# Mixture-of-experts decoder step on one core: where TensorE turns the next tile's gathered rows

## The reference, cut to what matters

```python
def hier_moe(h, rw1, rb1, rw2, rb2, w_gate, w_up, w_down):
    t = h.reshape(n * L, D)                       # D = 1024
    ...                                           # gates: two of 16 experts a token
    a = jnp.einsum('td,edf->tef', t, w_gate)      # f = 256
    b = jnp.einsum('td,edf->tef', t, w_up)
    hid = (jax.nn.silu(a) * b * gates[:, :, None].astype(a.dtype)).astype(t.dtype)
    out = jnp.einsum('tef,efd->td', hid, w_down)
    return out.reshape(n, L, D)
```

## Time and profile before

| | before |
|---|---|
| device time, three runs | 1176.96, 1177.94, 1178.39 us; median 1177.94 |
| span of the profiled execution | 1181.0 us |
| TensorE busy | 1083.1 us, 92% |
| VectorE busy | 777.0 us, 66% |
| ScalarE busy | 508.2 us, 43% |
| POOL busy | 295.5 us, 25% |
| the expert loop | about 728 to 1131 us |

### The profile page before, as it was taken

How to read it: one execution, slowest core, us unless ns; L and a number is a source line. 1 busy time by engine, 2 the same in 40 slices (tenths; PEclk the granted TensorE clock), 3 DMA queues, 4 the chain that set the end, 5 groups by cost and what they waited for, 6 DMA issues and landing times. The chain is left out here.

```text
span 1181.0 us, 18306 instructions
## 1 busy us (share of the span) xinstructions
PE 1083.1 (92%) x5541; PEld 804.7 (68%) x5542; DVE 777.0 (66%) x1276; ACT 508.2 (43%) x715; POOL 295.5 (25%) x359
## 2 busy tenths in 40 slices
PE   4799999999958899999999989999999999999992
PEld 2357777676646667777787646787878777778760
DVE  5456575756879973369887778555666555555385
ACT  5133242421132325436665344555555444444373
POOL 0046262616041000030000002333333323333344
PEclk9799999999989999999999989999999999999996
DMA  9834646557677459485766456897789777775597
GB/s 285 304 107 119 194 138 180 147 155 218 195 212 143 145 157 234 175 232 204 250 221 223 162 214 236 238 289 220 214 255 281 214 213 216 214 212 108 111 356 304
DMA packets 169247, 244.77 MB, mean 207 GB/s; under 512 B 66240, under 2 KB 124384, under 8 KB 167088
## 3 DMA queue, kind: packets, MB, share of 16 engines
q1 hardware_dynamic: 140833, 171.06, 45.8%
q0 software_dynamic: 16112, 54.88, 18.3%
q10 hardware_dynamic: 12246, 18.14, 4.6%
HBM read 169.36 MB, written 75.84 MB: 208 GB/s over the span
## 5 line engine op out<-in xcount | busy, mean ns | idle before, releaser
L126 PE MATMUL experts_psGU<-weights_we_hi,experts_x_hi 128*128 (+1 forms) x344 | 143.3, 417 | 2.7 <-issue 1.5
L128 PE MATMUL experts_psGU<-weights_we_lo,experts_x_hi 128*128 (+1 forms) x344 | 136.0, 395 | 0.0
L127 PE MATMUL experts_psGU<-weights_we_hi,experts_x_lo 128*128 (+1 forms) x344 | 135.9, 395 | 0.0
L126 PE MATMUL front_psM<-front_hT_hi,front_w_hi 128*128 128x512 f32 x256 | 107.0, 418 | 0.8 <-DVE front_hT_lo L1008 0.8
L128 PE MATMUL front_psM<-front_hT_lo,front_w_hi 128*128 128x512 f32 x256 | 101.5, 397 | 0.0
L127 PE MATMUL front_psM<-front_hT_hi,front_w_lo 128*128 128x512 f32 x256 | 101.5, 396 | 0.0
L2496 POOL DMA_INDIRECT acc_d<-experts_o_sb,experts_to_col x40 | 68.4, 1711 | 130.8 <-issue 64.8
L126 PEld LDWEIGHTS experts_psGU<-weights_we_hi,experts_x_hi 128*128 128x128 f32 x344 | 64.6, 188 | 28.5 <-issue 15.5
L2670 DVE TENSOR_TENSOR experts_x_lo<-experts_psX,experts_x_hi 128x1024 fp32r<-128x1024 f32 x42 | 51.4, 1225 | 37.5 <-ACT experts_x_hi L2560 37.5
L2660 DVE TENSOR_TENSOR weights_we_lo<-weights_we_raw,weights_we_hi (+1 forms) x64 | 75.5, 1221 | 0.0
L128 PEld LDWEIGHTS experts_psGU<-weights_we_lo,experts_x_hi 128*128 128x128 f32 x344 | 64.6, 188 | 15.5
(11 more groups left out here) (521 smaller groups left out, 2534.0 us busy)
## 6 DMA issues: line engine op xcount, KB each, us to landing
front_raw<-in_w_ada SPq DMA_DIRECT2D x32, 512.0 KB, 4.1
weights_we_raw<-in_exp_w_gate SPq DMA_DIRECT2D x16, 1024.0 KB, 6.0
weights_we_raw<-in_exp_w_up SPq DMA_DIRECT2D x16, 1024.0 KB, 12.5
weights_wd_raw<-in_exp_w_down SPq DMA_DIRECT2D x16, 1024.0 KB, 13.2
front_xraw<-in_x_prompt SPq DMA_DIRECT2D x4, 2048.0 KB, 10.7
front_raw<-in_w_ada SPq DMA_DIRECT2D x8, 1024.0 KB, 14.3
part_d<-middle_ev ACTq DMA_DIRECT2D x16, 512.0 KB, 3.0
middle_xt<-in_x_prompt SPq DMA_DIRECT2D x16, 512.0 KB, 4.7
```

The source lines that it names most:

```text
L126: pe.matmul(out, l_hi, r_hi, start=start, stop=False)
L127: pe.matmul(out, l_lo, r_hi, start=False, stop=False)
L128: return pe.matmul(out, l_hi, r_lo, start=False, stop=stop)
```

## The change

In the loop, `turn` for the next tile is no longer issued after `gate_up` and ahead of `down`, but in the middle of `gate_up`, right behind `turn_hidden`. Its two waits (for the gather, and for `x_lo` of the tile before) move with it. In tile 0, ahead of the loop, nothing changes. The number of instructions of every kind stays the same; ScalarE's, VectorE's, POOL's and SP's programs are untouched.

```diff
--- before.py
+++ after.py
@@ -2837,6 +2837,7 @@
                         turn(1, 1)
                     elif q == KD // 2:
                         turn_hidden(t - 1, 1 - u)
+                        turn(t + 1, 1 - u)
                     if isinstance(t, int) and q % 2 == 0:
                         pe.wait_ge(wlo, 4 * e + q // 2 + 1)
                     mm = matmul3(pe, psG[:, u, :], x_hi[:, u, q, :], x_lo[:, u, q, :],
@@ -2879,7 +2880,6 @@
                     u = 1 - d
                     s = t + d
                     gate_up(s, u, now)
-                    turn(s + 1, 1 - u)
                     down(s - 1, before)
                     before, now = now, after
             turn_hidden(last, 0)
```

## The result

| | before | after |
|---|---|---|
| median of four runs | 1178.16 us | 1189.31 us (1187.86 to 1190.68) |
| ratio to before, 95% interval | | 1.0081 (1.0065 to 1.0097) |
| span of the profiled execution | 1181.0 us | 1188.9 us |
| expert loop, first gate/up product of tile 1 to last of tile 42 | 402.9 us | 414.3 us |
| two tiles of the loop (medians of the two halves) | 9.68 + 9.59 us | 10.02 + 9.85 us |

Forecast: 1188.6 us, range 1184 to 1194. The two medians are 11.15 us apart, which is 0.95%; the ratio in the table is the one on record, and 1.0095 lies inside its interval.

The account below looks back on a forecast made before the run. The prediction took x_lo releasing every gate/up on TensorE as the bound. +11.1 us over 41 steps less 0.4 for jumps gave +10.7: span 1181.0 to 1191.7, less 3.1 for the median, 1188.6 us; range 1184 to 1194.

Parts of the forecast that it names:

- Busy share hides the bound: TensorE in the expert loop: 92% busy over the span, yet busy time covers up to 0.16 us of waiting between products.
- Every gate/up was released by x_lo already before: At gate/up's start in the loop before: x_lo, not the down products, releases it; 0.07 and 0.21 us lost.
- The turns cost 0.87 ahead of T wherever they stand: TensorE's eight turns a tile: 0.87 us, delaying T by that inside gate/up; sharing one place saves at most 0.02.
- T: The start of the last of a tile's 24 gate/up products on TensorE; other times are counted from it.
- x_hi gains only 0.60 because it stands behind silu: ScalarE behind gate/up: x_hi at T+0.71 instead of T+1.31, x_lo ended T+2.98, the next load 0.60 us earlier.
- +0.27 us a tile: Each loop tile: 0.87 us more ahead of T, 0.60 less behind it; over 41 steps +11.1 us.
- The give-back of up to 2.8 us: Loop's first half: the extra 0.14 us from x_lo to load might be hidden once x_lo is late, 20 x 0.14.
- The give-back of the longer jumps: Three jumps back take about 0.5 us more; overlapping the later x_lo hides 0 to 0.8 us, 0.4 taken.
- From the profile to the median: Whole run: profiled span 1191.7 us, less the 3.1 us by which the median lay below it, gives 1188.6 us.
- rival 4: TensorE in the loop: ten transposes in one stretch and waiting might cost the 2.4 GHz level; 1228 us, chance 0.02.
- The gather: Fetch of rows the turns need: still issued two tiles apart, some 19 us, landing within 8.2; priced at nothing.
- Rival 1: ScalarE in the loop: x_hi running before silu lets x_lo end in time; -6.6 us, 1171.3 us, chance 0.03.

Follow-up runs that it names:

- experiment 5: Kernel before, with gate/up starting on a wait for x_hi and the wait for x_lo behind its first product; loop 400.1 us, ratio to before 0.9979.
- experiment 4: Changed kernel with the next tile's turns ahead of the last three gate/up products instead of the middle; loop 413.6 us, ratio to before 1.0094.
- experiment 1: Changed kernel with x_hi ahead of silu on ScalarE and x_lo ahead of the gated product on VectorE; loop 397.6 us, ratio to before 0.9959.
- experiment 6: Changed kernel with only x_hi moved ahead of silu on ScalarE, VectorE's order left; loop 398.9 us, ratio to before 0.9952.
- experiment 8: Changed kernel with one more small ScalarE copy, its result unused, between silu and x_hi; loop 426.2 us, ratio to before 1.0186.
- experiment 7: Changed kernel with x_hi and x_lo first and the wait for x_lo behind gate/up's first product; loop 399.3 us, ratio to before 0.9966.
- 3: Changed kernel with the last two waits at gate/up's start swapped, the wait for x_lo now last; loop 412.5 us, ratio to before 1.0090.
- experiment 2: Changed kernel with gate/up starting on a wait for x_hi and the wait for x_lo behind its first product; loop 400.7 us, ratio to before 0.9973.

## Why the prediction was right

- *Busy share hides the bound.* Right. TensorE shows 92% before and after.
- *Every gate/up was released by x_lo already before.* Right for the regular tiles, by experiment 5: 9.50 instead of 9.68 and 9.59 us with the wait one product later.
- *The turns cost 0.87 ahead of T wherever they stand, and sharing a place saves at most 0.02.* Right: 1.09 for ten together, and 0.87 again for the eight that stand alone in experiment 4.
- *x_hi gains only 0.60 because it stands behind silu.* Right to 0.01 (T+0.71, x_lo ended T+2.97 to T+2.99), and shown to be the cause by experiments 1, 6 and 8. The Trainium skill, "TensorE: Matmul & The Clock Gate", section "Architectural detail: the array is 16x 32x32, not 1x 128x128", has ScalarE's queue as strictly first in, first out. The profile after agrees: ScalarE sits idle for 3.23 us in front of silu while turned rows lie ready for x_hi behind it.
- *+0.27 us a tile.* Measured 19.87 - 19.27 = 0.60 for two tiles, 0.30 a tile. The excess is the distance from x_lo to the load at the jump, 0.48 instead of 0.43: 1 us over the loop. The give-back of up to 2.8 us that the range allowed for this distance did not come.
- *The give-back of the longer jumps.* This term was mis-sized: forecast 0 to -0.8, -0.4 taken. All three are absent from the profile after, 1.7 us (10.19 + 10.36 + 10.19 less 3 x 9.68). They are not scattered by chance: in the profile before they stand ahead of tiles 11, 25 and 31, in experiment 5 ahead of 11, 23, 25 and 31, in experiment 7 ahead of 23, and experiments 1 and 6 have lesser ones of 0.16 to 0.26 us ahead of 25, and of 25 and 31. The kernels in which a late x_lo holds every tile (after, 3, 4 and 8) have none, and neither has experiment 2. Whether the change only hides them is not settled. In experiments 1 and 6 the load there comes 0.39 to 0.50 behind the last down product, which the 0.66 that x_lo asks for after the change would hide; in the profile before it comes 0.85 to 1.01 behind, which 0.66 would not. So two errors, +1.0 and -1.3 us, cancelled by luck.
- *From the profile to the median.* The prediction went from the span, 1191.7, to the median by taking off the 3.1 us that lay between them before. That did not carry over: after the change the span is 1188.9, the time of that same execution 1190.68 and the median 1189.31. The forecast is unharmed, because adding 10.7 to the median before gives the same number.
- *The clock (rival 4).* 1.00 in the loop with ten transposes in a row. The Trainium skill, "TensorE: Matmul & The Clock Gate", section "Part 4: PE-mode transpose", holds that transposes don't count as TensorE activity for the clock gate. If so, it changed nothing here; no run tells whether it holds.
- *The gather.* No wait for it appeared on TensorE.

Rival 1's time was out of reach by moving the turns alone, as its condition said; with ScalarE's order changed too it is experiment 1, and that or experiment 6 beats both kernels: 0.4 and 0.5% faster than before, with intervals from 0.3 to 0.7%.

Open: what makes the longer jumps (it is not the loading of instructions: the trace before has no such transfer between 750 and 1139 us), and why the distance at the jump grew by 0.05 (experiment 4 has 0.43, experiment 8 0.46, with the same order of waits).

## What to carry to other kernels

Moving work that an engine must do anyway from between two stages into one of them takes away cover: ask which chain ran behind it, and whether its consumer can use the earlier result at all, or stands in its own engine's queue behind something that needs the *end* of the stage. Move the producer and the consumer together, or neither. And compare starts, not busy shares, where the shown lengths of instructions overlap.

## What the hardware showed beyond that

- What TensorE's sequencer does between a wait and the first product it guards costs time when the wait is late: about 0.15 us for what experiment 3 moved, and 0.29 to 0.34 us from x_lo's end to the load for the rest. Behind the wait for `hid`, the turn followed 0.05 after its operand; the code has no address to work out there.
- In ten profiles tile 1 of the loop began between 723.2 and 728.8 us, behind a stretch with the same code in all (in experiments 2, 5 and 7 tile 1 itself waits less, which is 0.8 of it). That is half the size of the effect studied: one profile against one says little about 0.5% unless the changed stretch is compared by itself.
- On ScalarE an instruction starts 0.10 before the shown end of the one before, 0.28 after the start of a 0.38 us silu, also where a wait that is already fulfilled stands between.
